# A two-layer hybrid-attention block and its second block: conditioning rows moved from TensorE to VectorE, latent values moved into the drain of the stage before, and the next projections' inputs made before the last residuals

## The chip, the cores and the metric

The kernel runs on one core of one Trainium2 chip. The metric is the device time of one execution in microseconds (us). The core's engines are TensorE (PE; PEld is its weight load), VectorE (DVE), ScalarE (ACT), GpSimd (POOL) and SyncE (SP); each runs its own instruction list in order, and they meet only at semaphores.

## The reference

Sequence and model width are both 1024, everything is float32. The part that the change touches is the first block, two layers of this, and the input of the second block's first projection:

```python
def hybrid_layer(x, c, ...):                       # two layers, DEPTH = 2
    mod = jax.nn.silu(c) @ ada_w + ada_b           # [1, 1024] @ [1024, 3072]
    shift, scale, gate = jnp.split(mod, 3, axis=-1)
    h = rms_norm(x, norm_g) * (1.0 + scale[:, None, :]) + shift[:, None, :]
    proj = h @ w_in                                # queries, keys, values of three attentions, and gates
    ...                                            # latent, neighbourhood, differential attention
    y = jnp.concatenate([o_mla * silu(g_mla), o_na * silu(g_na), o_d * silu(g_diff)], axis=-1) @ w_out
    return x + gate[:, None, :] * y

# second block, first step
hn = rms_norm_2(h, ln)
proj = hn @ w_in
```

In latent attention keys and values are both projected from a 128-wide latent; `lt_v` below are its values, six heads of 64 = 384 columns.

## The kernel before, in words

Activations lie transposed: a tensor of 1024 x 1024 is 8 tiles (k or `tile`) of 128 features by 1024 positions, and the positions are worked in two halves (`hf`) of 512. A float32 product is made of three passes: each operand is split into a high part (ScalarE rounds it) and a low part (VectorE subtracts), and a group of 8 tiles x 3 = 24 matmuls of 128x512 makes one output tile of one half in one of the PSUM banks 0 to 3 (`i % 4`). The weights come in blocks of 1 MB on SP's queue (`streamed`), two buffers in turn; ScalarE rounds a block (`round_block`), VectorE makes its low part (`block_rest`), and TensorE waits for that at the group that opens it.

**The end of a layer** (`layer_end`, one function on each of three engines) has E = 32 groups: i = 0 to 15 are gates, i = 16 to 31 the output projection. Output tiles 0 and 1 come first half first; the last eight groups (i = 24 to 31) are tiles 4 to 7 of the first half, then tiles 4 to 7 of the second half, so the first half is complete after i = 27. After group i VectorE adds the residual into `h` and frees the bank, ScalarE starts the spill of that tile and half to memory and squares it, GpSimd adds the squares (`root_additions`). TensorE turns the sum of a half into the root's input (`root_sums`), ScalarE makes the root (`norm_root`), VectorE the normed tiles (`normed_tile`): for the first half this is at i = 28 and 29 of the same layer end. VectorE can be at most four groups behind, since group i waits for bank i - 4.

**Conditioning.** The vector `mod` of the next layer is made from 24 weight blocks; 8 of them at the start, 16 "late" ones inside layer 0's `layer_end`. ScalarE loads a late block into one of three slots (`ada_load`), TensorE multiplies it by a widened `silu(c)` (`ada_products`, 8 matmuls of 128x32 by 256 columns, recorded as 16), ScalarE copies the row out (`ada_row`), TensorE sums it over the partitions (`ada_sums`). `ADA_MAIN_AT` and `ADA_SUM_AT` give the group behind which each stands, in TensorE's list and in ScalarE's.

**The transition** to the next projections (`projected`; layer 1's, then those of the second block): ScalarE makes the high part of the normed input of the first half (`input_high`, or `rounded` before the second block), VectorE the low part, 8 tiles each. In ScalarE's list three of the eight high parts of layer 1 stand ahead of the last spill, in VectorE's list all low parts stand behind the last residual. TensorE's group 0 takes each tile as its low part arrives. Behind group 0 TensorE has `root_sums` of the second half, group 1 waits for that half's root, and the squares' sum of group v stands behind group v + 1. ScalarE squares group 0's result only when all eight high parts of the second half are made. Groups 0 to 3 are of the first half, group 4 is the first of the second.

**From differential to latent attention.** The differential stage has U = 32 units; TensorE's loop goes on to c = U + 3 to drain. Behind a barrier of all engines (`phase_end`) `latent` begins with 8 matmuls for `lt_v` into banks 0 to 7, which ScalarE copies out; then ScalarE squares the differential output (`m[:, 6]` and `m[:, 7]`, 128x1024 each) and only then squares the first latent chunk, which GpSimd adds (`squares_sum`) and TensorE sums (`latent_sums`).

## Time and profile before

| what | value |
|---|---|
| time, median of 3 runs | 4284.48 us (4276.0 to 4285.75) |
| the profiled execution's own time | 4271.69 us |
| its span, first to last instruction | 4269.9 us |
| mean granted TensorE clock | 0.981 |

The rows further down come from the profiled execution. Times in them are microseconds from the start of the span; "idle before" with an engine behind an arrow is time in which the engine waited, and for what. Matmuls overlap, so the pitch is the distance between their starts.

### The profile page before, as it was taken

How to read it: one execution, taken by the hardware profiler on the slowest of the kernel's cores; microseconds unless marked ns; L12 is line 12 of the kernel's file. 1: busy time of each engine (PE TensorE's matmuls, PEld its weight loads, DVE VectorE, ACT ScalarE, POOL GpSimd, SP SyncE). 2: the span in 40 equal slices, each digit the busy share in tenths (PEclk: the TensorE clock that was granted, in tenths of full speed). 3: DMA queues.
4: the chain of work that ended last, by engine and by line, in shares of the span. 5: the costliest groups of instructions: out<-in, count | busy, mean ns of one | idle time of the engine just before them, and what ended most of it. 6: DMA issues, size and time to landing. Idle time of an engine off the chain costs nothing.

```text
span 4269.9 us, 53415 instructions
## 1 busy us (share of the span) xinstructions
PE 4107.0 (96%) x22404; PEld 3089.1 (72%) x22404; DVE 1943.4 (46%) x2772; ACT 1566.7 (37%) x2408; POOL 552.0 (13%) x654
## 2 busy tenths in 40 slices
PE   7999989999999989999999799999999999999999
PEld 5776556777776556787833668888888888888887
DVE  3336956434336956433345743333334443333344
ACT  4326855323326855323356333121123231211231
POOL 0010111100010111110068810000002210000010
PEclk8999999999999999999999999999999999999999
DMA  4111000251111000032100101111111101111111
GB/s 161 58 62 43 1 1 1 89 188 50 58 62 43 1 1 1 21 111 69 40 11 1 43 30 50 50 50 50 50 50 70 40 20 50 50 50 50 50 65 64
DMA packets 47055, 208.33 MB, mean 49 GB/s; under 512 B 14688, under 2 KB 15328, under 8 KB 25568
## 3 DMA queue, kind: packets, MB, share of 16 engines
q1 hardware_dynamic: 31568, 144.98, 9.8%
q10 hardware_dynamic: 15248, 59.94, 3.9%
q8 instruction: 178, 2.92, 0.3%
q14 instruction: 61, 0.50, 0.0%
HBM read 188.12 MB, written 12.58 MB: 47 GB/s over the span
## 4 chain that ended last, share of the span: by engine, by line
PE 87%; DVE 6%; ACT 3%; issue 2%; DMA 1%; POOL 0%; ACTq 0%; DVEq 0%; POOLq 0%
PE ps L734 14%; PE ps L1305 13%; PE ps L1307 13%; PE ps L1306 13%; PE ps L1080 3%; PE ps L964 3%; PE ps L966 3%; PE ps L965 3%; PE ps L821 2%; PE ps L838 2%; PE ps L1036 2%; PE ps L1133 1%; PE ps L1021 1%; PE ps L1122 1%; PE ps L790 1%
## 5 line engine op out<-in xcount | busy, mean ns | idle before, releaser
L1305 PE MATMUL ps<-n_hi,w_hi 128*128 128x512 f32 x1280 | 500.1, 391 | 0.0
L1307 PE MATMUL ps<-n_hi,w_lo 128*128 128x512 f32 x1280 | 498.0, 389 | 0.0
L1306 PE MATMUL ps<-n_lo,w_hi 128*128 128x512 f32 x1280 | 498.0, 389 | 0.0
L1305 PE MATMUL ps<-m_hi,w_hi 128*128 128x512 f32 x1152 | 449.8, 390 | 0.0
L1307 PE MATMUL ps<-m_hi,w_lo 128*128 128x512 f32 x1152 | 448.2, 389 | 0.0
L1306 PE MATMUL ps<-m_lo,w_hi 128*128 128x512 f32 x1152 | 448.1, 389 | 0.0
L1451 ACT ACTIVATE w_hi<-w 128x2048 fp32r<-128x2048 f32 x103 | 196.9, 1912 | 443.0 <-DMA w<-in_wstream 442.8
L2106 DVE TENSOR_TENSOR w_lo<-w,w_hi 128x2048 fp32r<-128x2048 f32 x103 | 235.9, 2290 | 177.6 <-ACT w_hi L1451 177.6
L2016 ACT ACTIVATE arena<-ps 128x512 f32<-128x512 f32 x128 | 76.5, 598 | 585.3 <-PE ps L1307 585.3
L2826 DVE TENSOR_TENSOR m<-ps,arena 128x512 f32<-128x512 f32 x128 | 88.5, 692 | 433.5 <-ACT arena L2016 433.5
L1305 PEld LDWEIGHTS ps<-n_hi,w_hi 128*128 128x128 f32 x1280 | 240.3, 188 | 50.9 <-issue 1.2
L1306 PEld LDWEIGHTS ps<-n_lo,w_hi 128*128 128x128 f32 x1280 | 240.3, 188 | 50.8 <-issue 1.2
L1307 PEld LDWEIGHTS ps<-n_hi,w_lo 128*128 128x128 f32 x1280 | 240.3, 188 | 50.0
L1306 PEld LDWEIGHTS ps<-m_lo,w_hi 128*128 128x128 f32 x1152 | 216.3, 188 | 45.8 <-issue 1.0
L1305 PEld LDWEIGHTS ps<-m_hi,w_hi 128*128 128x128 f32 x1152 | 216.2, 188 | 45.6 <-issue 1.0
L1307 PEld LDWEIGHTS ps<-m_hi,w_lo 128*128 128x128 f32 x1152 | 216.3, 188 | 44.9
L734 PE MATMUL ps<-n_hi_m,w_lo 128*128 128x512 f32 x608 | 241.1, 397 | 0.0
L2236 DVE TENSOR_REDUCE small<-ps 128x1 f32<-128x1024 f32 x128 | 154.6, 1214 | 29.6 <-PE ps L1080 29.6
L3130 POOL TENSOR_TENSOR rope_cos<-rope_cos,arena 128x512 f32<-128x512 f32 x42 | 54.6, 1300 | 864.7 <-ACT arena L1976 864.4
L1745 ACT ACTIVATE h<-ps,small 128x1024 f32<-128x1024 f32 x128 | 142.7, 1115 | 53.0 <-DVE small L2236 52.8
L2290 DVE TENSOR_REDUCE small<-ps 128x1 f32<-128x1024 f32 x96 | 113.0, 1219 | 90.9 <-PE ps L826 90.9
L1604 ACT ACTIVATE arena<-ps,small 128x1024 f32<-128x1024 f32 x96 | 107.1, 1115 | 120.7 <-DVE small L2290 120.7
(393 smaller groups left out, 8142.5 us busy)
## 6 DMA issues: line engine op xcount, KB each, us to landing
w<-in_wstream SPq DMA_DIRECT2D x121, 1024.0 KB, 4.8
arena<-in_wstream ACTq DMA_DIRECT2D x17, 1024.0 KB, 5.2
out<-h ACTq DMA_DIRECT2D x48, 256.0 KB, 2.0
h<-in_na_bias ACTq DMA_DIRECT2D x6, 1152.0 KB, 6.7
h<-in_xT SPq DMA_DIRECT2D x2, 2048.0 KB, 12.5
m<-in_wstream SPq DMA_DIRECT2D x4, 1024.0 KB, 16.4
arena<-in_wstream SPq DMA_DIRECT2D x4, 1024.0 KB, 23.7
h<-in_xT ACTq DMA_DIRECT2D x4, 1024.0 KB, 10.6
```

Of the source, the lines that this page charges most:

```text
L734: last = mm(dst, a_part[:, k, wcols], b_part[:, tile0 + k, :], start=(k == 0 and b_part is hi and a_part is wb[0]), stop=(k == nk - 1 and ...
L964: mm(dst, wb[0][:, k, wcols], hi[:, k, :], start=(k == 0), stop=False)
L965: mm(dst, wb[0][:, k, wcols], lo[:, k, :], start=False, stop=False)
L966: last = mm(dst, wb[1][:, k, wcols], hi[:, k, :], start=False, stop=(k == KT - 1))
L1080: last = mm(ps[:, 2 * i + hf, :], q[r0:r0 + 32, t * P:t * P + P], k[r0:r0 + 32, hf * HALF:hf * HALF + HALF], start=True, stop=True)
L1305: mm(dst, wb[0][:, k, wcols], hi[:, k, :], start=(g == 0), stop=False)
L1306: mm(dst, wb[0][:, k, wcols], lo[:, k, :], start=False, stop=False)
L1307: last = mm(dst, wb[1][:, k, wcols], hi[:, k, :], start=False, stop=(g == KT - 1))
L1451: nc.scalar.activation(home[s][:, :], w[s][:, :], ACT.Copy).then_inc(sems["w_hi"], 1)
L1745: nc.scalar.activation(df_p[:, 2 * (c % 3) + i, :], psf[:, 2 * i * HALF:(2 * i + 2) * HALF], ACT.Exp, bias=negm[:, e:e + 1], accum_out=sum ...
L2106: V.tensor_tensor(out=w_lo[s][:, :], in0=x, in1=home[s][:, :].bitcast(F32), op=ALU.subtract)\
L2236: V.reduce_max(negm[:, u:u + 1], src, AX.X, negate=True).then_inc(sems["m_ready"], 1)
```

## The change

It has four parts.

1. **Late conditioning rows on VectorE.** `ada_products` and ScalarE's copy are gone from layer 0's end. VectorE multiplies a late block's 8 tiles of 128x256 by a column of `silu(c)` each and adds them up in a row (`ada_row`, one `tensor_scalar` and seven `scalar_tensor_tensor`, each waiting for the one before). The rows stand at new places, there are three row buffers, the sums and the loads that follow them are moved, the read of the modulation is moved from i = 7, 19, 25 to 13, 26, 31, and the load of layer 1's small table from i = 8 to 15.
2. **Latent values in the drain.** Four of the eight `lt_v` matmuls run in the drain of the differential stage (behind c = U - 1 and c = U + 1). One of the two 128x1024 squares moves on ScalarE to that drain, the other goes to GpSimd behind the barrier. The last turning of factors uses banks 2 and 3.
3. **Projections begun on first halves.** At i = E - 2 ScalarE makes all eight first-half high parts and VectorE all eight low parts, ahead of residuals 30 and 31. On TensorE `root_sums` of the second half stands behind group 1, and only the sum of group 1 waits for the root.
4. **Squares between high parts.** ScalarE squares group 0 ahead of the second half's root, and squares group 1 between the fourth and fifth high part; VectorE puts out group 0 between low parts 4 and 5.

```diff
-ADA_MAIN_AT = {2 + 3 * i // 2: i for i in range(len(ADA_LATE))}
-ADA_SUM_AT = {at + 1: i for at, i in ADA_MAIN_AT.items()}
-ADA_READ_AT = {7: 0, 19: 1, 25: 2}
+ADA_ROW_AT = {at: i for i, at in enumerate((3, 5, 7, 9, 12, 14, 16, 18, 19, 20, 22, 23, 24, 26, 27, 29))}
+ADA_SUM_AT = {at: i for i, at in enumerate((6, 8, 10, 12, 16, 17, 19, 20, 21, 22, 24, 25, 28, 29, 30, 31))}
+ADA_READ_AT = {13: 0, 26: 1, 31: 2}
+ADA_ROWS = 3
-INPUT_EARLY = 3
+NEXT_AT = E - 2
+FIRST_HALF_LAST = max(i for i, x in enumerate(END) if x.hf == 0)
...
 # TensorE, projected
-                        if i == 1:
-                            pe.wait_ge(sems["lay_rstd"], 2 * u + 2)
-                        if i == 0 and u:
+                        if i == 1 and u:
                             root_sums(u, 1)
                     v = i - 1
+                    if v == 1:
+                        pe.wait_ge(sems["lay_rstd"], 2 * u + 2)
...
 # TensorE, latent values
+            def latent_v(layer, t):
+                if t in (2, 3, 4, 5):
+                    pe.wait_ge(sems["lat_v_done"], NT * layer + t - 1)
+                mm(ps[:, t % 2 if t < 4 else t - 4, 0:384], lt_kv[:, t * P:t * P + P], lt_wv, start=True, stop=True)\
+                    .then_inc(sems["lat_v_full"], 1)
             def latent(layer):
-                pe.wait_ge(sems["lat_w"], 128 * (layer + 1))
-                for t in range(NT):
-                    mm(ps[:, t, 0:384], ...)
+                for t in range(4, NT):
+                    latent_v(layer, t)
...
 # TensorE, the differential stage's loop
+                        if c == U - 1:
+                            pe.wait_ge(sems["lat_w"], 128 * (layer + 1))
+                            pe.wait_ge(sems["exp_done"], T.since("exp_done", 2 * U - 1))
+                        if c in (U - 1, U + 1):
+                            for v in range(2):
+                                latent_v(layer, 2 * (c > U) + v)
                         if c == U + 1:
...
-                                factor_turns(LAT_PAIRS - 1, hf, hf)
+                                factor_turns(LAT_PAIRS - 1, hf, 2 + hf)
...
 # TensorE, layer_end: ada_products and its waits are gone
-                            ada_products(ada_slots[late % ADA_SLOTS], 6)
                         if layer == 0 and i == LAM_AT:
-                            pe.wait_ge(sems["ada_row"], ADA_FIRST + len(ADA_LATE))
                             lam_sums(1)
...
 # ScalarE, layer_end
-                        elif i == E - 1:
-                            act.wait_ge(sems["acc_ready"], ready + END_READY[-1])
-                            for k in range(INPUT_EARLY):
+                        elif i == NEXT_AT:
+                            act.wait_ge(sems["acc_ready"], ready + END_READY[FIRST_HALF_LAST])
+                            for k in range(KT):
                                 input_high(layer + 1, k, 0)
...
+                    if layer == 0 and i in ADA_SUM_AT and ADA_SUM_AT[i] + ADA_SLOTS < len(ADA_LATE):
+                        act.wait_ge(sems["ada_row"], ADA_FIRST + ADA_SUM_AT[i] + 1)
+                        ada_load(ADA_SUM_AT[i] + ADA_SLOTS)
...
 # ScalarE, the differential stage's loop, and latent
+                        if c in (U, U + 2):
+                            for v in range(2):
+                                latent_v(layer, 2 * (c > U) + v)
+                        if c == U + 1:
+                            act.wait_ge(sems["o_free"], T.since("o_free", NT))
+                            nc.scalar.activation(m[:, 0, :], m[:, 6, :], ACT.Square).then_inc(sems["lat_d_act"], 1)
-                for hp in range(2):
-                    nc.scalar.activation(m[:, hp, :], m[:, 6 + hp, :], ACT.Square).then_inc(sems["lat_d_act"], 1)
...
 # ScalarE, the beginning of a layer's projections
+                    round_block()
+                    step(0)
+                    if layer:
+                        norm_root(layer, 1)
+                    for k in range(KT):
+                        input_high(layer, k, 1)
+                        if k == 3:
+                            step(1)
...
 # VectorE
+            def ada_row(late):
+                count = ADA_FIRST + late
+                row, wb = ada_rows[:, count % ADA_ROWS, :], ada_slots[late % ADA_SLOTS]
+                dve.wait_ge(sems[f"ada_late{late % ADA_SLOTS}"], 16 * (late // ADA_SLOTS + 1))
+                dve.wait_ge(sems["ada_sum"], count + 1 - ADA_ROWS)
+                for k in range(KT):
+                    ...
+                        V.scalar_tensor_tensor(out=row, in0=wb[:, k, :], scalar=col, in1=row, op0=ALU.mult, op1=ALU.add)\
+                            .then_inc(sems["ada_row"], 1)
...
+                        for k in range(KT if i == NEXT_AT else 0):
+                            if layer < L - 1:
+                                input_low(k, 0)
+                            else:
+                                even_low(k, 0)
                         dve.wait_ge(sems["acc_ready"], ready + END_READY[i])
...
+                    if layer == 0 and i in ADA_ROW_AT:
+                        ada_row(ADA_ROW_AT[i])
...
 # GpSimd, behind the barrier
+                G.tensor_tensor(out=m[:, 1, :], in0=m[:, 7, :], in1=m[:, 7, :], op=ALU.mult).then_inc(sems["lat_d_act"], 1)
```

The beginning of the second block's projections is rearranged in the same way as that of layer 1.

## Rows read from the trace of the kernel before

**Rows 1.** The page, parts 1 and 4: TensorE's line, and the chain by engine.

```profile
PE 4107.0 (96%) x22404; PEld 3089.1 (72%) x22404; DVE 1943.4 (46%) x2772; ACT 1566.7 (37%) x2408; POOL 552.0 (13%) x654
...
PE 87%; DVE 6%; ACT 3%; issue 2%; DMA 1%; POOL 0%; ACTq 0%; DVEq 0%; POOLq 0%
```

**Rows 2.** Windows: layer ends and transitions; the column header, then a stretch each.

```profile
core 0: us, PE busy (x) PEld busy (x) DVE busy (x) ACT busy (x) POOL busy (x), PEclk, DMA share, GB/s
...
798.70:1001.40 202.70, 202.66 (x1095) 158.43 (x1092) 70.51 (x96) 49.35 (x75) 15.55 (x12) 1.00 0.44 159
...
1001.40:1042.00 40.60, 31.09 (x103) 22.88 (x104) 22.27 (x28) 18.57 (x28) 2.56 (x2) 0.83 0.12 39
...
1758.40:1933.50 175.10, 175.10 (x773) 144.43 (x771) 68.45 (x81) 43.91 (x57) 15.52 (x12) 1.00 0.24 87
...
1933.50:1971.20 37.70, 29.10 (x104) 21.62 (x104) 21.48 (x29) 17.50 (x28) 2.56 (x2) 0.86 0.13 42
```

**Rows 3.** Timeline of TensorE (start, us, what): conditioning inside layer 0's end.

```profile
900.57 0.50 PE L940 MATMUL ps<-mats,arena 128*128 128x1 f32 x4
...
907.59 0.50 PE L940 MATMUL ps<-mats,arena 128*128 128x1 f32 x4
...
913.63 1.07 PE L932 MATMUL ps<-arena 128*32 128x256 f32 x16
...
920.25 0.50 PE L940 MATMUL ps<-mats,arena 128*128 128x1 f32 x4
```

**Rows 4.** Timeline of VectorE and GpSimd: 128x256 operations one after another.

```profile
560.38 0.48 DVE L2230 SCALAR_TENSOR_TENSOR arena<-ps,c_tmp,h 128x256 f32<-128x256 f32 x1 [11.32 <-ACT h L1443]
...
560.83 0.73 POOL L2949 TENSOR_TENSOR h<-h,m 128x256 f32<-128x256 f32 x1 [2.00 <-ACT h L1588]
...
560.90 0.94 DVE L2264 TENSOR_TENSOR arena<-arena,h 128x256 f32<-128x256 f32 x1
```

**Rows 5.** DMA issues of layer 0's end: KB each, median us to landing.

```profile
arena<-in_wstream ACTq DMA_DIRECT2D x16, 1024.0 KB, 5.1
...
h<-in_xT ACTq DMA_DIRECT2D x4, 1024.0 KB, 10.6
```

**Rows 6.** Timeline of TensorE in both transitions.

```profile
1003.79 0.47 PE L734 MATMUL ps<-n_hi_m,w_hi 128*128 128x512 f32 x1 [2.43 <-DVE n_lo L2375]
...
1015.54 0.47 PE L734 MATMUL ps<-n_hi_m,w_hi 128*128 128x512 f32 x1 [1.44 <-ACT arena L1443]
...
1026.30 2.07 PE L790 MATMUL ps<-arena,mats 128*128 128x512 f32 x2 [5.08 <-ACT arena L1568]
...
1041.99 1.02 PE L790 MATMUL ps<-arena,mats 128*128 128x512 f32 x2
...
1971.18 1.02 PE L790 MATMUL ps<-arena,mats 128*128 128x512 f32 x2
```

**Rows 7.** Timeline of VectorE in both transitions.

```profile
997.75 2.29 DVE L2106 TENSOR_TENSOR w_lo<-w,w_hi 128x2048 fp32r<-128x2048 f32 x1 [0.15 <-ACT w_hi L1451]
...
1002.40 6.94 DVE L2375 SCALAR_TENSOR_TENSOR n_lo<-n,mod,n_hi_m 128x512 fp32r<-128x512 f32 x8 [0.25 <-ACT n_hi_m L1547]
...
1015.42 1.41 DVE L2164 SCALAR_TENSOR_TENSOR n<-h,gain,arena 128x512 f32<-128x512 f32 x2 [3.88 <-ACT arena L1443]
...
1923.47 6.41 DVE L2164 SCALAR_TENSOR_TENSOR n<-h,g,arena 128x512 f32<-128x512 f32 x8
```

**Rows 8.** Timeline of ScalarE: the last second-half high part.

```profile
1025.04 0.72 ACT L1547 ACTIVATE n_hi_m<-n,mod 128x512 fp32r<-128x512 f32 x1 [0.60 <-DVE n L2164]
```

**Rows 9.** Timeline of TensorE and ScalarE where latent attention begins.

```profile
541.26 1.09 PE L1122 MATMUL ps<-arena 128*64 128x128 f32 x16 [1.95 <-ACT arena L1786]
...
549.26 5.40 PE L879 MATMUL ps<-arena 128*128 128x384 f32 x16 [0.53 <-DVEq L2090]
...
555.08 1.99 ACT L1629 ACTIVATE m<-m 128x1024 f32<-128x1024 f32 x2
...
558.29 1.19 PE L808 MATMUL ps<-h,mats 128*128 128x256 f32 x2 [2.77 <-POOL h L2949]
```

More of the change, by code:

```diff
@@ L1519, in layer_end @@
                     else:
-                        if i == E - 1 and layer == L - 1:
+                        if i == NEXT_AT and layer == L - 1:
                             act.wait_ge(sems["spilled0"], 128 * L)
@@ L1688, in _ @@
                 with T.span(**LAYER_COUNTS.totals):
-                    for hf in range(H2):
-                        if hf and layer:
-                            norm_root(layer, 1)
-                        for k in range(INPUT_EARLY if layer and hf == 0 else 0, KT):
-                            input_high(layer, k, hf)
-                        if hf == 0:
-                            round_block()
                     def at_block(b):
@@ L1837, in evict @@
                                              ACT.Copy).then_inc(sems["acc_free"], 1)
[L1839 removed]
+                step = projected(EVEN_COUNTS, [w_hi] + [w_hi_m] * 7, lambda g: sb_tmp, {"q": 1.0 / SB_D, "k": 1.0 / SB_D}, at_block, evict)
+                round_block(w_hi_m)
+                step(0)
+                norm_root(L, 1)
+                act.wait_ge(sems["spilled1"], 128 * L)
+                for k in range(KT):
+                    rounded(k, 1)
+                    if k == 3:
+                        step(1)
+                for i in range(2, EVEN_COUNTS.n + 1):
+                    step(i)
             phase_end()
@@ L2144, in modulation @@
                 dve.wait_ge(sems["v_link"], T.next("v_link"))
+            def ada_row(late):
[3 more added lines that the diff above has]
+                dve.wait_ge(sems["ada_sum"], count + 1 - ADA_ROWS)
+                for k in range(KT):
+                    col = c_silu[:, k:k + 1]
+                    if k == 0:
+                        V.tensor_scalar(row, wb[:, k, :], col, None, ALU.mult).then_inc(sems["v_link"], 1)
+                    elif k < KT - 1:
+                        V.scalar_tensor_tensor(out=row, in0=wb[:, k, :], scalar=col, in1=row, op0=ALU.mult, op1=ALU.add)\
+                            .then_inc(sems["v_link"], 1)
+                    else:
+                        V.scalar_tensor_tensor(out=row, in0=wb[:, k, :], scalar=col, in1=row, op0=ALU.mult, op1=ALU.add)\
+                            .then_inc(sems["ada_row"], 1)
+                    if k < KT - 1:
+                        dve.wait_ge(sems["v_link"], T.next("v_link"))
             def modulation_read(i):
@@ L2372, in _ @@
                 with T.span(**LAYER_COUNTS.totals, x_split=2 * KT):
-                    def input_low(k, hf):
-                        dve.wait_ge(sems["x_hi"], T.next("x_hi"))
-                        V.scalar_tensor_tensor(out=half(n_lo, k, hf), in0=half(n, k, hf), scalar=shift[:, k:k + 1],
-                                               in1=half(n_hi_m, k, hf).bitcast(F32), op0=ALU.add, op1=ALU.subtract)\
-                            .then_inc(sems["x_split"], 1)
-                    for k in range(KT):
+                    for k in range(0 if layer else KT):
                         input_low(k, 0)
@@ L2383, in _, with group_out @@
                         dve.wait_ge(sems["rope_in"], 32)
-                    for k in range(KT + 1):
-                        if k < KT:
-                            normed_tile(layer, k, 1)
-                        if k:
-                            input_low(k - 1, 1)
                     C = LAYER_COUNTS
-                    for i, g in enumerate(C.groups):
+                    def group_out(i, g):
                         if i in C.converts:
@@ L2419, in _ @@
                             V.tensor_copy(lt_pe[64:96, cols], ps[64:96, i % 4, :]).then_inc(sems["acc_free"], 1)
+                    for k in range(KT + 1):
+                        if k < KT:
+                            normed_tile(layer, k, 1)
+                        if k:
+                            input_low(k - 1, 1)
+                        if k == 5:
+                            group_out(0, C.groups[0])
+                    for i in range(1, C.n):
+                        group_out(i, C.groups[i])
                     V.tensor_copy(picks[0:MLA_QK, 0, :].rearrange("p (j n) -> p j n", j=2),
@@ L2548, in _ @@
                            sb_tmp[2][:, i % 2, :], "acc_free")
+                for k in range(KT + 1):
+                    if k < KT:
+                        normed_tile(L, k, 1)
+                    if k:
+                        even_low(k - 1, 1)
+                    if k == 5:
+                        group_out(0, C.groups[0])
+                for i in range(1, 16):
+                    group_out(i, C.groups[i])
                 block_rest(w_hi_m)
```

107 lines of the change are left out of this document (48 added, 59 removed).

## The prediction

> **What bounds the kernel now.** I read the page first. TensorE is busy 96% of the span and makes 87% of the chain that ended last; VectorE is busy 46%, ScalarE 37% [rows 1]. So a microsecond counts only if it leaves TensorE's list or closes a gap in it. Then I took windows over the places that the diff touches [rows 2]. Layer 0's end takes 202.7 us and layer 1's, the same 32 groups without conditioning, 175.1; in both TensorE never rests. The stretches behind them hold gaps: in 40.6 us TensorE is busy 31.1, in 37.7 us 29.1, and the granted clock averages 0.83 and 0.86, so part of the busy time ran at the lower of its two levels. TensorE's own timeline names the waits [rows 6]: 2.43 us for the first low part, 1.44 for the second half's root, 5.08 for the square of group 0, which ScalarE makes only behind the eighth high part [rows 8]. The last place is the beginning of latent attention, where TensorE waits 2.77 us for GpSimd, GpSimd for ScalarE, and ScalarE squares 128x1024 twice, 1.99 us, right before [rows 9].
>
> **Part 1, conditioning rows.** A plain group takes 5.44 us (175.1 less 0.9 for one root sum, over 32). The pitches of [rows 3] give the breaks: a sum with products 907.59 - 900.57 = 7.02, a sum alone 913.63 - 907.59 = 6.04, products alone 920.25 - 913.63 = 6.62; so 1.58, 0.60 and 1.18 us over a plain group. Two rows need one of each, 3.36 us, and 16 rows 26.9; the difference of the two layer ends is 27.6, the other 0.7 is the small sum for lambda and what surrounds it. After the change the 16 sums stand alone, 15 inside the layer end (9.0 us) and one behind group 31. With the 0.7 that is 9.7.
> The change adds one wait. `lam_sums` stands behind group 26 on TensorE and needs what `first_tables` makes on VectorE; that was at i = 19 and is now at i = 26, behind residual 26. A residual costs 0.74 (a 128x512 of the same kind, 1.41 for two, [rows 7]), with two small steps 1.0 us. Group 27 and all behind it wait. Gain: 27.6 - 9.7 - 1.0 = **16.9 us**, and the new layer end is 185.8 long.
> What hides the rows is VectorE's slack. A row is eight 128x256 operations in series. The nearest rows are 0.48 us for such an operation with a start 0.52 later for the next [rows 4]; I take 4.0 us a row (seven at 0.52, the first a little less). The bounds are 3.8 (0.48 each) and 7.5 (0.94 each, the longest there). At 4.0 VectorE has 70.5 + 64 = 134.5 us of work in 185.8, and where rows are densest, three in four groups, 3 x 4.0 + 4 x 0.75 + 2.3 for a block's low part = 17.3 of 24.2. From 6.3 us a row it would fall behind there.
> The row operation waits for its load; behind it on VectorE stand residuals and `block_rest`, for which TensorE waits, residuals with four groups of room. The tightest lead is row 9 at i = 20, loaded from i = 19: one group, 6.0, less residual, spill and square, about 1.0, against 5.1 us to landing [rows 5], so about level. Row 7 at i = 18 is loaded from i = 16 behind the four loads of `h`, which land in 10.6: two groups, 11.5. Neither costs TensorE anything. Row 15 at i = 29 is on the path, see below. ScalarE's new wait before a load is for a row at least one group old; behind it stand spills and squares. It loses 16 copies. The table's load has until i = 26. SP's queue is untouched, and so is its pace, as it waits for TensorE's groups.
>
> **Parts 3 and 4, the transitions.** Call T the end of the last group of the layer end (1001.4 and 1933.5). The mark is the start of the sum of group 2, behind which TensorE has no gap: T + 40.6 and T + 37.7 [rows 6].
> Into layer 1, VectorE: group 29 ends at T - 12.1 (two groups, two sums), residual to -11.3, row 15 to -7.3, eight normed tiles at 0.67 to -2.0, the block's low part 2.29 [rows 7] to +0.3, first low part +1.0. GpSimd's addition can hold it: in layer 1's end the eight normed tiles took 6.41 instead of 5.3 [rows 7], so I take T + 2.0. ScalarE's high parts are ready by then. Group 0 is then fed at 0.67 a tile and eats 0.68: T + 7.4. Group 1: 12.9. Residuals 30 and 31 come at about T + 8, their squares and additions by T + 11, so `root_sums` runs at once, to 13.8, the sum of group 0 to 14.7, group 2 to 20.1. The root is out at 15.1. The fourth high part and the square take 5.6: the sum of group 1 starts at 20.7, group 3 ends at 27.0. The eighth high part came 10.3 us behind the first normed tile [rows 7, 8]; with ScalarE's inserted square and root 1.9 more, with group 2's square 0.6: 27.9. Gain: 40.6 - 27.9 = 12.7.
> Into the second block there is no row and no sum: normed tiles end at T - 3.6 [rows 7], the low part of the block at -1.1, so group 0 starts at T. By the same steps group 2 ends at 18.1, group 3 at 24.9, the last square at 25.5. Gain: 37.7 - 25.5 = 12.2. Together **24.9 us**. The lower clock of these stretches is in the old marks; the new gaps are under 1 us each, so I count it away. Price if it stays: some 13 matmuls at 0.2 us more, 2.6 a transition.
> Bounds: from 12 (VectorE's work comes late and half of it is waited for elsewhere) to 28 (no collision, no wait at all but the last square's).
>
> A rule of the Trainium skill speaks against this part and part 1. First the row: a VectorE operation of two SBUF inputs took 0.94 us beside a GpSimd addition, its neighbour 0.48 [rows 4]. The skill's page SBUF — State Buffer, section Who interferes with whom, says that a VectorE instruction with two SBUF inputs contends with a GpSimd one that reads SBUF, and that one of them is blocked for the whole instruction; by this, the trace agrees. Seven of eight operations of a row and all normed tiles are of that kind. By the rule the first low part of layer 1 comes up to 1.1 us later than without it; without it the sum would be 1.0 larger.
>
> **Part 2, latent values.** One `lt_v` matmul pair costs 0.65 us (eight from 549.26 to about 554.5). Two run in the 1.95 us gap before 541.26, free. Two stand before the last turning of factors: 1.3 less the 0.24 gap behind, so the barrier comes 1.05 later, at 550.3. Behind it four cost 2.6: 552.9; first latent product, ScalarE's square to 554.0, GpSimd 0.73 [rows 4]: first sum at 554.9 instead of 558.29 [rows 9]. GpSimd's own square (1024 columns) is at most four times the 0.73 of 256, 2.9, done at 553.2, in time. ScalarE's moved copies and square lie in its waits of that drain. Gain 3.4 a layer, **6.8 us** for both; bounds 2 (GpSimd late by 2.4) and 8.
>
> **The sum.** 16.9 + 24.9 + 6.8 = 48.6 us. Against the profiled execution's 4271.7 that gives 4223; against the median of the runs, 4284.5, which lies 12.8 above it, 4236. The runs spread from 4276.0 to 4285.75. I put the forecast between, at 4231.
>
> **Rivals.**
> - *The wait moves inside the transitions.* VectorE now has row, normed tiles, block, low parts and only then residuals 30 and 31. If it runs 5 us later than I count, group 0 starves and groups 2 and 3, which wait for these residuals' banks, follow. For it: low parts were the first wait before [rows 6]. Against: it is idle for a third of the layer end. Gain 36: 4235 to 4248, 4243 on the middle.
> - *Rows are dear.* At 0.94 us an operation a row takes 7.5, 16 of them 120, with 70.5 more than the stage. Part 1 gives nothing, row 15 falls onto the transition and takes its gain too; 12.2 + 6.8 stay: 4259. For it: [rows 4]'s stretched operation. Against: GpSimd is busy 15.6 of 202.7 us [rows 2].
> - *Slower than before.* VectorE bound by rows alone: 70.5 + 16R must exceed 185.8 + 48.6, so R over 10.2 us, 1.28 an operation. At R = 12 the layer end is 263 us and the time about 4310. No row is near.
> - *Latent values gain nothing*, as GpSimd's square is in the way: 4238.
>
> **Chances.** The forecast, with part 2 or not, 0.77; the moved wait 0.15; dear rows 0.05; slower 0.03. A measurement here tells about 0.3%, 13 us, from no change: faster by more than that 0.94, within it 0.03, slower 0.03. The range goes from 4212 (28 for the transitions, against the profiled time) to 4256, which takes in the moved wait.
>
> **What would show it.** In the new profile TensorE has no products inside layer 0's end, which lasts 184 to 188 us, with 16 sums and one wait of about 1 us behind group 26; VectorE's row operations are near 0.5 us and none makes TensorE wait; the sum of group 2 starts about 28 and 25.5 us behind T at a clock near 1; the first latent sum comes some 5 us behind the barrier instead of 9. The prediction is wrong if row operations pass 0.8 us, if TensorE waits for a block's low part or for a row's load in layer 0's end, or if group 0 starts later than T + 4.

## The result, and the profile after

The changed kernel takes 4220.3 us (median of 4 runs, 4215.42 to 4223.53) where the kernel before took 4282.3 beside it (4 runs, 4276.0 to 4285.75): ratio 0.9856, 95% interval 0.9839 to 0.9873, 62 us faster. The profiled execution is the fastest of the four: 4215.42 us, span 4213.6, against a span of 4269.9. So 56.3 us lie between the two profiles, where the sum said 48.6.

The page, parts 1 and 4, against [rows 1]:

```profile
PE 4074.4 (97%) x22148; PEld 3077.3 (73%) x22148; DVE 2001.6 (48%) x2898; ACT 1557.4 (37%) x2390; POOL 556.7 (13%) x656
...
PE 87%; DVE 6%; ACT 3%; issue 2%; DMA 1%; POOL 0%; SPq 0%; ACTq 0%; DVEq 0%; POOLq 0%
```

TensorE has 32.6 us less to do (some of it is clock, not work) and VectorE 58.2 more; the shape of the chain is the same. The windows over the four stretches of [rows 2], from T on to the start of the sum of group 2 (columns as in [rows 2]):

```profile
787.29:971.62 184.33, 183.43 (x838) 151.69 (x836) 131.28 (x219) 48.83 (x66) 15.67 (x12) 1.00 0.48 174
971.62:999.12 27.50, 25.15 (x107) 19.34 (x106) 21.74 (x30) 12.66 (x20) 2.58 (x2) 1.00 0.16 58
1711.39:1886.65 175.26, 175.26 (x774) 144.82 (x773) 69.23 (x83) 47.69 (x65) 15.54 (x12) 1.00 0.24 87
1886.65:1911.58 24.93, 24.52 (x102) 18.92 (x102) 18.27 (x27) 12.51 (x20) 2.60 (x2) 1.00 0.18 64
```

Layer 0's end went from 202.7 to 184.3 us, the transitions from 40.6 to 27.5 and from 37.5 to 24.9 with the clock up from 0.83 and 0.86 to 1.00; layer 1's end, which nothing touched, is the same to a tenth. TensorE's timeline inside layer 0's end and behind it, against [rows 3, 6]:

```profile
911.14 0.50 PE L947 MATMUL ps<-mats,arena 128*128 128x1 f32 x4
...
917.09 0.50 PE L947 MATMUL ps<-mats,arena 128*128 128x1 f32 x4
...
941.43 0.38 PE L953 MATMUL ps<-lam,mats 32*128 32x2 f32 x2 [0.90 <-DVE lam L2140]
...
973.64 0.47 PE L736 MATMUL ps<-n_hi_m,w_hi 128*128 128x512 f32 x1 [1.68 <-DVE n_lo L2220]
```

A group with a sum has a pitch of 5.95 us; the wait for lambda's tables is there at 0.90; group 0 of layer 1 starts 2.0 us behind T. VectorE's timeline, against [rows 4, 7], and below it GpSimd's over the first of these rows:

```profile
899.45 0.75 DVE L2259 SCALAR_TENSOR_TENSOR h<-ps,mod,h 128x512 f32<-128x512 f32 x1 [0.27 <-PE ps L973]
900.12 0.34 DVE L2180 TENSOR_SCALAR arena<-arena,c_silu 128x256 f32<-128x256 f32 x1
900.50 3.99 DVE L2182 SCALAR_TENSOR_TENSOR arena<-arena,c_silu 128x256 f32<-128x256 f32 x6
904.52 0.48 DVE L2185 SCALAR_TENSOR_TENSOR arena<-arena,c_silu 128x256 f32<-128x256 f32 x1
...
908.53 0.35 DVE L2180 TENSOR_SCALAR arena<-arena,c_silu 128x256 f32<-128x256 f32 x1 [2.38 <-DMA arena<-in_wstream]
908.92 3.09 DVE L2182 SCALAR_TENSOR_TENSOR arena<-arena,c_silu 128x256 f32<-128x256 f32 x6
...
965.24 5.38 DVE L2208 SCALAR_TENSOR_TENSOR n<-h,gain,arena 128x512 f32<-128x512 f32 x8
970.54 2.29 DVE L2131 TENSOR_TENSOR w_lo<-w,w_hi 128x2048 fp32r<-128x2048 f32 x1
972.75 5.39 DVE L2220 SCALAR_TENSOR_TENSOR n_lo<-n,mod,n_hi_m 128x512 fp32r<-128x512 f32 x8
```

```profile
901.34 1.31 POOL L2973 TENSOR_TENSOR arena<-arena 128x512 f32<-128x512 f32 x1 [9.48 <-ACT arena L1465]
```

The one of the six operations that began inside it, in a window of VectorE's timeline for itself:

```profile
901.54 1.39 DVE L2182 SCALAR_TENSOR_TENSOR arena<-arena,c_silu 128x256 f32<-128x256 f32 x1
```

A row takes 4.0 us (0.35, then seven at a pitch of 0.52), and 4.9 with a GpSimd addition in it (six operations in 3.99 instead of 3.09). The beginning of latent attention, TensorE and GpSimd, against [rows 9]:

```profile
544.96 2.82 PE L881 MATMUL ps<-arena 128*128 128x384 f32 x8 [0.53 <-DVEq L2115]
...
549.58 0.67 PE L810 MATMUL ps<-h,mats 128*128 128x256 f32 x2 [0.94 <-POOL h L3010]
```

```profile
545.34 1.89 POOL L3019 TENSOR_TENSOR m<-m 128x1024 f32<-128x1024 f32 x1 [6.81 <-DVEq L2115]
```

**A place that the prediction did not have.** Windows over layer 0's own projections, first matmul to the sum of group 2, before and after:

```profile
53.64:86.56 32.92, 29.43 (x100) 22.49 (x101) 18.97 (x26) 11.50 (x16) 0.00 (x0) 0.80 0.00 1
```

```profile
51.58:77.97 26.39, 26.39 (x101) 20.86 (x102) 18.98 (x26) 11.13 (x16) 0.00 (x0) 0.89 0.00 1
```

The same work in 6.5 us less. Of all stretches that the diff touches:

| stretch | before | changed | gain | predicted |
|---|---|---|---|---|
| layer 0's projections, to the sum of group 2 | 32.92 | 26.38 | 6.5 | none |
| end of the last differential scores to the first latent sum, both layers | 21.03 + 21.05 | 17.60 + 17.60 | 6.9 | 6.8 |
| layer 0's end | 202.67 | 184.33 | 18.3 | 16.9 |
| T to the sum of group 2, layer 1 | 40.63 | 27.50 | 13.1 | 12.7 |
| the same, second block | 37.54 | 24.93 | 12.6 | 12.2 |
| together | 355.84 | 298.33 | 57.5 | 48.6 |
| the rest of the span | 3914.1 | 3915.3 | -1.2 | 0 |

The experiments below are read by this table, since their sum repeats to 0.1 us (last experiment) and the time of a whole run only to some 10. Each stretch is read from one profiled execution per kernel.

### The profile page after: what moved, and what is told of

Read it like the earlier page. It is cut to its first block, busy times and chain, and to the rows that moved or that the text cites. A ratio compares the mean times of both kernels' runs of the same rounds, so it can differ in the third digit from the quotient of the medians.

```text
span 4213.6 us, 53001 instructions
## 1 busy us (share of the span) xinstructions
PE 4074.4 (97%) x22148; PEld 3077.3 (73%) x22148; DVE 2001.6 (48%) x2898; ACT 1557.4 (37%) x2390; POOL 556.7 (13%) x656
## 4 chain that ended last, share of the span: by engine, by line
PE 87%; DVE 6%; ACT 3%; issue 2%; DMA 1%; POOL 0%; SPq 0%; ACTq 0%; DVEq 0%; POOLq 0%
PE ps L736 14%; PE ps L1308 13%; PE ps L1310 13%; PE ps L1309 13%; PE ps L1077 3%; PE ps L971 3%; PE ps L973 3%; PE ps L972 3%; PE ps L823 2%; PE ps L840 2%; PE ps L1033 2%; PE ps L1130 2%; PE ps L1018 1%; PE ps L1119 1%; PE ps L1048 1%
## 6 DMA issues: line engine op xcount, KB each, us to landing
h<-in_xT SPq DMA_DIRECT2D x2, 2048.0 KB, 12.2
```

## Experiments

Times are medians beside runs of the kernel before on the same chip, where it took 4271 to 4272 us. All edits are made to the changed kernel.

**One part undone at a time.** `e1_rows_back` gives layer 0's end its products, copies and places of before.

```
 ADA_MAIN_AT = {2 + 3 * i // 2: i for i in range(len(ADA_LATE))}
 ADA_SUM_AT = {at + 1: i for at, i in ADA_MAIN_AT.items()}
...
+                            ada_products(ada_slots[late % ADA_SLOTS], 6)
...
-                    if layer == 0 and i in ADA_ROW_AT:
-                        ada_row(ADA_ROW_AT[i])
```

> The changed kernel with part 1 alone undone: the conditioning rows of layer 0's end are TensorE products with ScalarE's copies again, at their old places. Theory (the terms of the sum hold one by one): layer 0's end is 202 to 203 us long again instead of 184.2; as VectorE has no row behind residual 29, group 0 of layer 1 starts at T instead of T + 2.2 and the sum of group 2 at about T + 25.5 instead of T + 27.7. Net 18.5 - 2.2 = 16.3 us slower than the changed kernel: 4237 us, that is 46 faster than before. Rival (rows on VectorE press on the transition more than counted, so that their true worth is smaller): the sum of group 2 comes at T + 22 or earlier, and the time is 4232 or less. Rival (part 1 also carries what the prediction did not account for, 7.7 us): 4244.

Measured: 4232.7 us, ratio 0.9905 (0.989 to 0.992), 38 faster than before. The layer end is 202.65 us, group 0 of layer 1 starts at T - 0.2, the sum of group 2 at T + 25.2; together 16.0 longer than changed. The theory holds to 0.3 us in the stretches; the time lies at the edge of what it allows.

`e2_layer0_order` keeps the old order in layer 0's projections alone.

```
-                    step(0)
+                    step(0) if layer else None
...
-                        if k == 3:
+                        if k == 3 and layer:
                             step(1)
+                    if not layer:
+                        step(0)
+                        step(1)
```

> The changed kernel with the new order undone in layer 0's own projections alone, which the prediction never priced: there ScalarE squares groups 0 and 1 behind the eighth high part of the second half again; the two transitions keep the new order. Theory (this place is most of the 7.7 us that the prediction lacked): TensorE waits some 3.5 us for ScalarE's square ahead of the first sums again, three times in one row, and the sum of group 1 comes 6.5 us later behind the first projection than now; the time is 4220 + 6.5 = 4227, 55 to 56 under before. Rival (the 7.7 us are only a spread from run to run, and the place is worth nothing, since the time is given back before the first barrier): 4220, 62 under before, and the first barrier as far behind the first projection as now.

Measured: 4224.9 us, 0.989 (0.9872 to 0.9908), 46 faster. The stretch is 32.78 us again, 6.4 longer, and nothing gives it back before the first barrier. TensorE's timeline there:

```profile
68.87 2.08 PE L794 MATMUL ps<-arena,mats 128*128 128x512 f32 x2 [3.68 <-ACT arena L1570]
```

That one wait is 3.7 us; the other 2.7 lie behind it, up to the next sum, at the lower clock: over the stretch the granted clock averages 0.81, in the changed kernel 0.89. In the changed kernel TensorE comes out of its first wait, 6.64 us, at the lower level (matmuls 0.43 us apart), reaches the upper one (0.23 apart) after 13 matmuls and does not fall again.

`e3_latent_back` puts all eight latent values and both squares behind the barrier, the squares on ScalarE.

```
-                for t in range(4, NT):
+                for t in range(NT):
                     latent_v(layer, t)
+                for hp in range(2):
+                    nc.scalar.activation(m[:, hp, :], m[:, 6 + hp, :], ACT.Square).then_inc(sems["lat_d_act"], 1)
...
-                G.tensor_tensor(out=m[:, 1, :], in0=m[:, 7, :], in1=m[:, 7, :], op=ALU.mult).then_inc(sems["lat_d_act"], 1)
```

> The changed kernel with part 2 alone undone: all eight latent values and both squares of 128x1024 behind the barrier again. Theory: TensorE waits 2.8 us for GpSimd ahead of the first latent sum instead of 0.9, the first sum comes about 9 us behind the barrier instead of 5, and each layer is 3.4 us longer: 4227 us, 55 under before. Rival (the clock or other work gives the gain back behind the first sum): 4220. Rival (a longer wait there also costs clock behind it, as the changed kernel gained another 1.7 us between 584 and 606 us of its span): 4230.

Measured: 4222.5 us, 0.9895 (0.9863 to 0.9927), 49 faster; the time alone cannot tell the theories apart. The stretch can: 21.03 and 21.05 us again, 3.4 longer a layer, with the wait of before:

```profile
554.69 1.19 PE L810 MATMUL ps<-h,mats 128*128 128x256 f32 x2 [2.77 <-POOL h L2999]
```

`e4_transitions_back` undoes both halves of parts 3 and 4 in the two transitions.

```
-NEXT_AT = E - 2
+NEXT_AT = E - 1
+INPUT_EARLY = 3
...
-                        if i == 1 and u:
+                        if i == 0 and u:
                             root_sums(u, 1)
...
-                        for k in range(KT if i == NEXT_AT else 0):
-                            if layer < L - 1:
-                                input_low(k, 0)
-                            else:
-                                even_low(k, 0)
```

> The changed kernel with parts 3 and 4 undone in the two transitions alone (high and low parts of the first halves begun behind the last group, squares of groups 0 and 1 behind the eighth high part of the second half); layer 0's projections keep the new order. Theory: the sum of group 2 comes at T + 40 or more and T + 37.7 instead of T + 27.7 and T + 25.2, the granted clock there is near 0.85 again, and the time is 4220 + 12.9 + 12.4 = 4246, 37 under before. In layer 1 it may be 1 us more, since row 15 stands behind residual 29 on VectorE. Rival (the gains of transitions and rows overlap: with the old order row 15 falls onto the path as a whole): sum of group 2 at T + 44 in layer 1 and 4250 or more. All four parts undone one by one should sum to 56 to 62.

Measured: 4242.9 us, 0.9931 (0.9917 to 0.9946), 28 faster. Windows from T to the sum of group 2:

```profile
976.75:1016.44 39.69, 28.55 (x107) 21.42 (x106) 24.05 (x31) 18.84 (x28) 2.55 (x2) 0.91 0.12 40
1903.00:1940.53 37.53, 29.17 (x103) 21.78 (x103) 21.52 (x29) 17.16 (x28) 2.55 (x2) 0.86 0.13 43
```

24.8 us longer, as expected, and row 15 is not dearer than counted (the rival wanted T + 44). The four undone parts sum to 16.0 + 6.4 + 6.9 + 24.8 = 54.1 of 57.5 us. 1.0 of the rest is e4's layer 1, shorter than before's because the clock stood at 0.91 and not 0.83; 2.3 is the earlier start of group 0 that e1 got back.

**Which half of a transition.** `e8_old_squares` keeps the early first halves and puts the squares behind the eighth high part; `e9_old_halves` does the opposite. Both leave TensorE's list as changed: `root_sums` of the second half behind group 1. e4 has it behind group 0.

```
 # e8, ScalarE, both transitions
-                step(0)
                 norm_root(L, 1)
...
                     rounded(k, 1)
-                    if k == 3:
-                        step(1)
+                step(0)
+                step(1)
...
 # e9
-NEXT_AT = E - 2
+NEXT_AT = E - 1
+INPUT_EARLY = 3
```

> The changed kernel with one half of the transitions undone: ScalarE squares groups 0 and 1 behind the eighth high part of the second half again, and VectorE reads out group 0 behind all normed tiles; the first halves are still begun while the last residuals run. Layer 0 keeps the new order. Theory (the order of the squares carries nearly all of a transition, since the sum of group 0 would wait for the eighth high part, 10 us behind a root that comes at about T + 15): the first sum at T + 25 to 26 with a wait of some 11 us ahead of it, the sum of group 2 at T + 38 in layer 1 and T + 36 in the second block; 22 us longer than the changed kernel, 34 under before. Rival (the order is worth what it was in layer 0, 6.5 us a place, and the early first halves the rest): 13 longer, 44 under before.

> The changed kernel with the other half of the transitions undone: high and low parts of the first halves begun behind the last group as before, three high parts early; the squares of groups 0 and 1 keep their new places. Theory (the new order of the squares carries most of a transition by itself, since the early halves alone gave nothing): group 0 starts at T + 5.0 in layer 1, behind row 15, and T + 2.3 in the second block; it is fed as in the run with both halves undone and ends 7.2 later; group 1, the root sum and the sum of group 0 follow without a wait for the eighth high part. Sum of group 2 at T + 32 and T + 29.5, instead of 27.5 and 24.9, and 39.7 and 37.5 with both undone. 9 us longer than the changed kernel, some 48 under before. Rival (each half is needed by the other): sum of group 2 at T + 37 or later.

Windows of e8, then of e9, T to the sum of group 2:

```profile
974.60:1016.89 42.29, 27.39 (x107) 20.78 (x106) 23.69 (x32) 14.81 (x22) 2.60 (x2) 0.84 0.10 38
1904.12:1942.29 38.17, 26.45 (x104) 20.00 (x103) 19.06 (x28) 13.75 (x21) 2.59 (x2) 0.82 0.11 42
```

```profile
977.18:1009.14 31.96, 26.67 (x105) 20.48 (x106) 23.11 (x30) 17.42 (x27) 2.55 (x2) 0.95 0.14 50
1896.93:1926.15 29.22, 26.41 (x104) 20.34 (x104) 20.79 (x28) 16.09 (x27) 2.56 (x2) 0.94 0.17 55
```

| T to the sum of group 2, us | old squares | new squares |
|---|---|---|
| old first halves | 39.7, 37.5 | 32.0, 29.2 |
| early first halves | 42.3, 38.2 | 27.5, 24.9 |

With old first halves the new places of the squares are worth 7.7 and 8.3 us. With the old squares the early first halves lose 2.6 and 0.6 us against e4. ScalarE's timelines of e4, then of e8, show the second half's root in layer 1:

```profile
990.49 0.63 ACT L1449 ACTIVATE arena<-arena 128x512 f32<-128x512 f32 x1
```

```profile
990.32 0.63 ACT L1446 ACTIVATE arena<-arena 128x512 f32<-128x512 f32 x1
```

That is T + 13.7 in e4 and T + 15.7 in e8, 2.0 later; in the second block T + 11.2 and T + 12.4. In e8 GpSimd has the squares added up at T + 12.1 and T + 7.9, but `root_sums` start only behind group 1, without a wait, at T + 14.0 and T + 10.7. The eighth high part follows the root and the old square follows that, so the sum of group 0 comes at T + 27.3 instead of T + 25.3 and at T + 23.5 instead of T + 22.2, although groups 0 and 1 end sooner and TensorE waits 12.2 us. The remaining 0.6 us, longer in layer 1 and shorter in the second block, stands behind that sum, where TensorE runs at the lower level for more matmuls or fewer. So the table does not part either edit alone from the place of `root_sums`, since e4 differs from e8 and from e9 in it too: with `root_sums` behind group 0 and the early halves kept, no run was made. With the new squares, early halves give 4.5 and 4.3 us more at the same place of `root_sums`. For e9 the stretches came within 0.3 us of the theory; e8 came out 4.3 and 2.2 us worse than its theory, at a clock of 0.84 and 0.82; it is 28.0 us longer than the changed kernel in the two stretches, where the theory said 22 and the rival 13. e8 took 4251.9 us (0.9945, 0.9923 to 0.9966), and its profiled execution lost 10 to 13 us elsewhere, see below; e9 took 4233.1 (0.9905, 0.9882 to 0.9928).

**How much cover VectorE has.** Each row gets more operations at its head.

```
-                for k in range(KT):
+                for k in [*range(4), *range(KT)]:   # e5; range(7) in e6, range(2) in e11
```

> The changed kernel with four operations more in each conditioning row (its first four are done, then the row is begun anew; the result is the same): a row of 4.0 us beside an idle GpSimd becomes 6.1, and 4.9 becomes 7.0. Theory (the prediction's cover: VectorE has room for rows until about 6.3 us where they stand in three of four groups): the last half falls behind. Counting VectorE's list group by group, layer 0's end becomes 191 instead of 184 us and group 0 of layer 1 starts near T + 5 instead of T + 2; together 8 to 9 us longer than the changed kernel, 47 to 50 under before. Rival (the room is larger, as TensorE has four groups of lead): at most 2 us longer, and the layer end stays at 184.3.

> The same with seven operations more in each row, 7.6 us beside an idle GpSimd and 8.5 beside its additions. Theory: VectorE's list alone, 70.5 us and 16 rows of 8, is 198 us and more, longer than TensorE's 184.3; counted group by group the layer end becomes 209 us and group 0 of layer 1 starts near T + 8. Together 28 to 32 us longer than the changed kernel, 25 to 30 under before. Rival (cover as large as 10 us a row, the prediction's bound for slower than before): less than 10 longer.

> The changed kernel with two operations more in each conditioning row: 5.0 us, and 5.9 beside GpSimd's additions, where four more made 17 us. Theory (a threshold near 6.3 us a row): the layer end stays within 2 us of 184.3 and group 0 of layer 1 starts a microsecond later; 2 to 4 us longer together. Rival (there is no room left: every 0.1 us of a row costs 0.8 from the start): 8 to 9 longer.

| row, us (beside an addition) | layer 0's end | T to the sum of group 2 | longer than changed | time, ratio |
|---|---|---|---|---|
| 4.0 (4.9), changed | 184.3 | 27.5 | | |
| 5.0 (5.9), e11 | 186.7 | 32.2 | 7.1 | 4228.3, 0.9898 (0.9872 to 0.9924) |
| 6.1 (7.0), e5 | 195.9 | 33.1 | 17.2 | 4230.1, 0.9903 (0.9882 to 0.9925) |
| 7.6 (8.5), e6 | 212.3 | 40.2 | 40.6 | 4259.3, 0.9974 (0.9961 to 0.9987) |

Windows of the same two stretches of e11, then of e6:

```profile
793.14:979.85 186.71, 183.49 (x838) 151.75 (x836) 142.92 (x248) 46.17 (x62) 15.52 (x12) 1.00 0.47 172
979.85:1012.04 32.19, 27.39 (x108) 20.98 (x106) 24.18 (x33) 15.32 (x24) 2.59 (x2) 0.89 0.13 49
```

```profile
790.04:1002.29 212.25, 192.73 (x835) 156.36 (x833) 172.65 (x314) 44.38 (x58) 15.64 (x12) 0.96 0.41 152
1002.29:1042.50 40.21, 27.81 (x106) 21.47 (x107) 32.17 (x47) 17.79 (x27) 2.60 (x2) 0.83 0.11 40
```

The loss does not begin at 6.3. Two operations more already cost 7.1 us, nearly what the rival of that run said, though the layer end alone grows by only 2.4 there and by 11.6 at the next step. TensorE's waits in e11 over its layer end and the start of group 0:

```profile
PE ps L736 <- DVE n_lo L2220: 4.1, 1, 4.1
PE ps L953 <- DVE lam L2140: 2.1, 1, 2.1
PE ps L971 <- DVE w_lo L2131: 1.1, 1, 1.1
```

VectorE's and ScalarE's timelines of e11 say what the first of these is:

```profile
965.82 0.41 ACTq L1484 DMA_DIRECT2D arena<-in_wstream  x1
```

```profile
971.09 0.35 DVE L2180 TENSOR_SCALAR arena<-arena,c_silu 128x256 f32<-128x256 f32 x1 [2.34 <-DMA arena<-in_wstream]
```

ScalarE issues row 15's load only behind the spill of residual 28, which VectorE had made late. The row waits 2.3 us for it, and normed tiles, the block's low part and group 0 wait behind the row. In the changed kernel the same load is issued at 954.97 and the row begins at 960.43, 5.5 us later, with no wait, against a median landing time of 5.2. So the 7.1 us of e11 are three things: 2.4 in the layer end (waits for lambda's tables and a block's low part), 2.4 by which group 0 starts later behind T, and 2.2 of clock: behind the wait of 4.1 us TensorE runs 11 matmuls at the lower level (0.43 us apart instead of 0.23), behind the changed kernel's 1.7 us none.

**Using that.** `e7_rows_earlier` issues each load one group behind the row that frees its slot, moves row 15 from i = 29 to 28 and lambda's tables from 26 to 20. `e10_square_sooner` adds the square of group 1 behind the third high part.

```
-... 22, 23, 24, 26, 27, 29))}
+... 22, 23, 24, 26, 27, 28))}
+ADA_LOAD_AT = {at + 1: i + 3 for at, i in ADA_ROW_AT.items() if i + 3 < len(ADA_LATE)}
+TABLES_AT = 20
...
+                    if layer == 0 and i == TABLES_AT:
+                        first_tables(1)
 # e10 besides
-                        if k == 3:
+                        if k == 2:
                             step(1)
```

> The changed kernel with each later row's load issued one group behind the row that frees its slot, and not behind its sum; row 15 behind residual 28 instead of 29; the tables of layer 1 at i = 20 instead of 26. Theory: the wait of 0.9 us ahead of the small sum for lambda goes, layer 0's end becomes 183.4 us; VectorE ends the normed tiles some 4 us earlier, so group 0 of layer 1 starts at T - 0.2 as in the second block, and the sum of group 2 comes at T + 25. Together about 3 us under the changed kernel, below what the times tell, but plain in the stretches of the profile. Rival (row 15 behind residual 28 delays residual 29 and the root's chain): group 0 early, but the sum of group 2 not earlier than T + 27.

> The run with the earlier rows, and in it the square of group 1 behind the third high part of the second half instead of the fourth, at all three places. Theory: the last waits of the transitions, 0.66 and 0.41 us ahead of the sum of group 1, go, and the sum of group 2 comes at T + 25.0 in layer 1 (25.7 with the earlier rows alone) and T + 24.5 in the second block (24.9); layer 0's start stays. 1.1 us under the run with the earlier rows, 3.9 under the changed kernel by the stretches. Rival (the fourth and later high parts, one square later, are late for group 2 and group 3): the sum of group 2 not earlier than now.

Windows of e7, layer 0's end and T to the sum of group 2; then of e10, with the second block:

```profile
789.63:972.97 183.34, 183.34 (x838) 151.68 (x836) 136.60 (x223) 48.57 (x66) 15.98 (x12) 1.00 0.48 175
972.97:998.65 25.68, 25.02 (x107) 19.26 (x106) 18.27 (x26) 12.82 (x20) 2.60 (x2) 1.00 0.18 62
```

```profile
791.49:974.85 183.36, 183.36 (x838) 151.68 (x836) 136.32 (x223) 48.62 (x66) 15.97 (x12) 1.00 0.48 175
974.85:1000.45 25.60, 24.91 (x105) 19.25 (x105) 18.19 (x26) 12.75 (x20) 2.60 (x2) 1.00 0.18 62
1888.32:1912.87 24.55, 24.41 (x103) 18.81 (x102) 18.15 (x27) 12.17 (x20) 2.61 (x2) 1.00 0.18 65
```

e7 is 2.8 us shorter over the two: TensorE is busy in all 183.34 us of the layer end, and group 0 starts 0.2 behind T. e10's square removes the wait ahead of the sum of group 1 in both places (0.8 and 0.6 us against e7 and against the changed kernel), but the way from that sum to the next is 0.7 and 0.2 longer, in layer 1 by a new wait of 0.69 us for the next square; net 0.1 in layer 1, as its rival said, and 0.4 in the second block, as its theory did. All edits together: 3.3 us of stretches. The times, 4217.3 (0.9879, 0.9858 to 0.990) and 4213.8 (0.9859, 0.9835 to 0.9883), cannot tell them from the changed kernel.

**The changed kernel again.**

> The changed kernel once more, unaltered, on the chip of these runs. Theory (the times move by several microseconds where TensorE's granted clock falls behind a thinly filled stretch, at another place in each execution; elsewhere stretches repeat to 0.1 us): the stretches that the change touches repeat to 0.2 us (layer 0's end 184.3, sums of group 2 at T + 27.5 and T + 24.9, 1.96 us from the first latent product to its sum), while the two local attention stages of each layer differ by 1 to 3.5 us, in either direction, at other granted clocks. 52 to 62 under before.

Measured: 4217.3 us, 0.9866 (0.9843 to 0.9888), 55 faster. The touched stretches sum to 298.24 against 298.33. Of the rest, differential attention of layer 1 is 3.1 us shorter, and the last 860 us are 9.7 longer, at one place. Windows of the changed kernel and of its repetition there:

```profile
3393.00:3433.00 40.00, 40.00 (x192) 33.06 (x191) 16.34 (x20) 15.24 (x25) 5.82 (x5) 1.00 0.08 27
```

```profile
3390.00:3430.00 40.00, 40.00 (x168) 34.41 (x168) 13.36 (x17) 13.08 (x20) 7.33 (x6) 0.76 0.00 0
```

The same code: 192 matmuls against 168, partly of other shapes, at a granted clock of 0.76. e8 and e10 show it too; the other eleven profiles of this study do not. Where the drop begins is shown at the end.

## Why the prediction was right, and where it was not

*The direction and the place of the gain* were right: 48.6 us in four terms, three of them measured within 0.5 us, and 57.5 us in all. 4231 was 10.7 over the median. Part of that closeness is the choice of a base between two values: from the median of before alone the sum gives 4236, 15.7 over. The 62 us are also the largest of the measured gains; the repetition, beside other runs of before, gave 55.

*The range* is looser than its words. Its low end, 4212, is said to be the sum with 28 us for the transitions against the profiled time, but 16.9 + 28 + 6.8 = 51.7, and 4271.7 less that is 4220. The measured 4220.3 would lie at its very edge. The 8 us below have no term in the text; that they covered a place which the sum had missed is luck.

*The missed place* is the largest error, 6.5 of 8.9 us. "Parts 3 and 4, the transitions" priced the order of the squares only behind the two layer ends. The diff rewrote `projected` and its callers for every layer, and layer 0's own projections wait for the same square; before's list of waits had three of these at one line, not two. e2 shows it: undone there alone, 6.4 us.

*Part 1, the sums.* Sum alone at 0.60 us over a plain group was mis-sized: from one pitch of 6.04 in [rows 3], where a group with products stood next to it. With no products it is 5.95 - 5.44 = 0.51 us; the 15 sums inside the layer end are 1.3 us of the 1.4 between 16.9 and 18.3, and the added wait, 0.90 for a predicted 1.0, is the rest.

*Part 1, the cover.* The row was right to the hundredth, 4.0 us, with 0.9 more beside an addition; VectorE's work in the layer end, 131.3, was near the 134.5 predicted. "From 6.3 us a row it would fall behind" was wrong: at 5.0 (5.9 beside an addition) TensorE already waits for a block's low part and 2.1 us for lambda's tables. The count took VectorE's slack as time that a row can fill, but much of it is not: VectorE waits 11.6 us there for block high parts and 25.7 for ScalarE's sigmoids. The rule also left out that loads hang on residuals by ScalarE's queue. The prediction had the tightest load at row 9, which did wait (2.38 us, hidden), and not at row 15, whose lateness nothing hides. The rival "rows are dear" put the loss at 7.5 us a row at 29.6 us (19 left of 48.6); e6, at 7.6 to 8.5 us a row, lost 40.6 and keeps 17 of 57.5. "Slower from 10.2 us" was not reached by any run; three operations more between e5 and e6 cost 23.4 us, so an estimate from these two runs puts the point near 8.7 us a row, 9.6 beside an addition.

*The transitions.* T + 27.5 and T + 24.9 for 27.9 and 25.5; group 0 at T + 2.0 as said. GpSimd's addition fell on row 15 (4.9 us) and not on the normed tiles (5.38 for eight), which is the same for group 0. The clock was counted away, and is 1.00. The text treats early first halves, squares and the place of `root_sums` as one; e8 shows that the first and the last without the squares lose.

*The rule on two SBUF inputs.* One operation in a row took 1.39 us and its neighbours 0.48, while a GpSimd addition ran 1.31. Taken by the letter, the prediction's sign of being wrong, "if row operations pass 0.8 us", was met: 7 of the 128 passed it, at a mean of 0.52. Six have two 128x256 inputs in SBUF and took 1.39 to 1.40; the seventh is a `tensor_scalar`, which has only one, and took 1.45 instead of 0.34. The Trainium skill, SBUF — State Buffer, section Who interferes with whom, has one of two such instructions blocked for the whole of the other; by this the trace agrees, and the size is one addition, not a stretch of all eight operations. For that reason the prediction's upper bound of 0.94 for every operation of a row was too high, though a single one can pass it.

*Latent values* were 3.43 us a layer for a predicted 3.4. GpSimd's square took 1.89 us, under its bound of 2.9, and ended 1.5 us before GpSimd's first addition could begin.

*The wait moves inside the transitions* did not occur: residuals 30 and 31 began at T + 6.4, against T + 8 counted.

## What to carry to other kernels

Read a diff by function before pricing it by place: an order that is changed in a helper acts wherever the helper is called, and the list of waits says how often. Slack of a helper engine is not room: add operations to the moved work and see what each costs, because loads, low parts and small tables hang on its queue and come late long before its busy time fills. Two edits to one chain are priced in all four combinations, and nothing else may differ between them; here early first halves gained 4.3 to 4.5 us a place on top of the new squares and lost 0.6 and 2.6 without them, and that loss came with a third edit, the later place of `root_sums`. And where whole runs spread by 10 us, compare the stretches that the change touches, which repeated to 0.1 here.

## What was not expected of the hardware

TensorE's granted clock falls at a few places, in some executions of the same code and not in others. The whole runs spread with it: of the four executions of e3 the shortest, 4214.3 us, has a mean granted clock of 0.988 and the longest, 4242.7, of 0.980. In neighborhood attention of layer 0 (106.9 us before, 110.0 changed, 108.1 to 109.8 in the others) it drops behind the stage's thin beginning. Windows of the changed kernel, then of before, each some 8 to 12 us into the stage:

```profile
301.60:305.60 4.00, 3.11 (x12) 1.80 (x12) 1.57 (x7) 2.68 (x5) 4.00 (x3) 0.50 0.00 0
```

```profile
310.00:314.00 4.00, 3.71 (x36) 2.66 (x38) 2.30 (x8) 3.05 (x8) 4.00 (x3) 1.00 0.01 4
```

12 matmuls at the lower level, 1.2 GHz, against 36 at the upper; the level accounts for a factor of two, the rest is that the changed kernel's profile is already behind here. In layer 1 it is the kernel before that has the drop (110.2 against 106.7). The diff has no edit in this stage; but in layer 0 the one profile of before is shorter than all thirteen others, and one profile cannot tell whether that is chance. The Trainium skill, TensorE: Matmul & The Clock Gate, section HAM oscillation — how this bites in real kernels, describes throughput lost to a clock that falls in kernels with idle gaps on TensorE; these stages have them.

The drop near the end in three profiles begins behind such a gap as well. TensorE's timeline of the repetition, and a window right behind it:

```profile
3379.32 0.46 PE L1406 MATMUL ps<-arena,m 128*128 128x128 f32 x2 [1.05 <-DVE m L2936]
```

```profile
3383.00:3387.00 4.00, 4.00 (x21) 4.00 (x20) 1.41 (x2) 1.56 (x3) 0.73 (x1) 0.50 0.02 4
```

In all three the same wait of 1.05 us for VectorE ends 2.2 to 2.4 us before the clock falls, and it then stays at the lower level for some 27 us in which TensorE is busy. The first profile of the changed kernel has the same wait of 1.05 us, which ends at 3382.39, and no drop: from 3386 to 3390 us it makes 38 matmuls at a clock of 1.00, where the repetition makes 21. So the wait alone does not decide it. What does, in one execution and not in the next, stays open.
